# Gates made head by head, and the gates of one of five dense token blocks added in DRAM by indirect DMA

## What is computed

```python
q = (xb @ w_q).reshape(t, PEER_HEADS, 2, PEER_HALF)
s = jnp.einsum('thpd,hpkd->thpk', q, sub_keys)
s1, i1 = lax.top_k(s[:, :, 0], PEER_TOPK)          # 8 heads, 16 of 128 keys in each half
s2, i2 = lax.top_k(s[:, :, 1], PEER_TOPK)
...                                                # the best 16 of the 16 x 16 sums: top_s, idx
gate = jax.nn.softmax(top_s, axis=-1)
act = jax.nn.gelu(jnp.einsum('thkd,td->thk', jnp.take(expert_u, idx, axis=0), xb))
return jnp.einsum('thk,thkd->td', gate * act, jnp.take(expert_v, idx, axis=0))
```

## Time and profile before

| | |
|---|---|
| timed runs | 2938.82 us median of 3 (2930.64 to 2947.14) |
| profiled execution | span 2939.3 us; no time of its own is listed beside the span |
| busy | PE 2830.0 us (96%), DVE 2512.5 (85%), ACT 885.5 (30%), POOL 1029.0 (35%) |
| DMA | 917.54 MB, mean 312 GB/s |
| queues | q1 (SP) 37.3% of 16 engines, q0 (POOL) 36.4%, q10 (ACT) 7.9% |

### The profile page before, as it was taken

How to read it: one execution, slowest core, us unless ns; L and a number is a source line. 1 busy time by engine, 2 the same in 40 slices (tenths; PEclk the granted TensorE clock), 3 DMA queues, 4 the chain that set the end, 5 groups by cost and what they waited for, 6 DMA issues and landing times. The chain is left out here.

```text
span 2939.3 us, 47358 instructions
## 1 busy us (share of the span) xinstructions
PE 2830.0 (96%) x19184; PEld 1834.9 (62%) x19184; DVE 2512.5 (85%) x4708; ACT 885.5 (30%) x1321; POOL 1029.0 (35%) x778
## 2 busy tenths in 40 slices
PE   4999999998999999999999999999999999999998
PEld 4566686766667877677776677777544444444443
DVE  6876556987887879999999999998699999999877
ACT  3333532221111432222222344444222222222223
POOL 0000000002776025444554532222456566655410
PEclk9999999999999999999999999999999999999999
DMA  8989653433999458888888999999999999999972
GB/s 328 348 318 381 238 199 129 144 123 115 391 392 378 192 215 288 303 325 314 330 315 320 354 327 346 350 346 341 368 398 405 405 388 414 407 401 404 364 267 115
DMA packets 222971, 917.54 MB, mean 312 GB/s; under 512 B 20208, under 2 KB 61216, under 8 KB 181536
## 3 DMA queue, kind: packets, MB, share of 16 engines
q1 hardware_dynamic: 61664, 427.91, 37.3%
q0 software_dynamic: 110592, 402.70, 36.4%
q10 hardware_dynamic: 50496, 83.89, 7.9%
HBM read 771.79 MB, written 142.63 MB: 311 GB/s over the span
## 5 line engine op out<-in xcount | busy, mean ns | idle before, releaser
L1718 PE MATMUL psU<-hB,w 128*128 128x320 f16 (+2 forms) x3104 | 927.4, 299 | 27.4 <-ACT Z L753 15.9
L1719 PE MATMUL psU<-hB,w 128*128 128x320 f16 (+2 forms) x3104 | 927.3, 299 | 0.0
L1720 PE MATMUL psU<-hB,w 128*128 128x320 f16 (+2 forms) x3104 | 927.0, 299 | 0.0
L753 ACT ACTIVATE w<-stage 128x2048 f16<-128x2048 f32 x176 | 335.7, 1909 | 606.1 <-PE psX L1720 331.2
L1043 DVE SCALAR_TENSOR_TENSOR w<-stage,w 128x2048 f16<-128x2048 f32 x176 | 402.3, 2287 | 99.4 <-ACT w L753 99.4
L746 POOL DMA_INDIRECT rows<-in_u_rows,idx_sp x200 | 267.8, 1339 | 376.0 <-DVE rows L1139 233.5
L1718 PEld LDWEIGHTS psU<-hB,w 128*128 128x128 f16 x3104 | 304.9, 98 | 140.2 <-issue 22.9
L1720 PEld LDWEIGHTS psU<-hB,w 128*128 128x128 f16 x3104 | 305.1, 98 | 117.6
L1719 PEld LDWEIGHTS psU<-hB,w 128*128 128x128 f16 x3104 | 305.0, 98 | 110.4
L746 POOL DMA_INDIRECT rows<-in_v_rows,idx_sp x205 | 271.4, 1324 | 285.4 <-DVE rows L1139 184.5
L1718 PE MATMUL psX<-w,Z 128*128 128x512 f16 x768 | 292.2, 381 | 7.6 <-DVE Z L1641 4.2
(11 more groups left out here) (263 smaller groups left out, 4435.8 us busy)
## 6 DMA issues: line engine op xcount, KB each, us to landing
stage<-in_u_units SPq DMA_DIRECT2D x64, 1024.0 KB, 8.8
stage<-in_v_units SPq DMA_DIRECT2D x64, 1024.0 KB, 8.0
stage<-in_w_front SPq DMA_DIRECT2D x48, 1024.0 KB, 8.6
hl_dram<-w SPq DMA_DIRECT2D x48, 1024.0 KB, 6.5
w<-hl_dram SPq DMA_DIRECT2D x48, 1024.0 KB, 7.2
a_dram<-R ACTq DMA_DIRECT2D x64, 640.0 KB, 8.0
...
Z<-a_dram SPq DMA_DIRECT2D x32, 1280.0 KB, 11.8
```

The lines of the kernel that those rows point to most:

```text
L753: return nc.scalar.activation(dst, src, func, scale=scale)
L1718: mm(ps, lhs[0](k), rhs[0](k), start=start and s == 0, stop=False)
L1719: mm(ps, lhs[0](k), rhs[1](k), start=False, stop=False)
L1720: last = mm(ps, lhs[1](k), rhs[0](k), start=False, stop=stop and s == n - 1)
```

## The change

Set B's five blocks are parted. Four of them (512 tokens, `NV`) keep the spreading by one-hots, now in 16 units, E44 to E59 (`E_SPREAD` = 44, `N_SPREAD` = 16). The last block (`DS` = 1, 128 tokens) gets its gates by adding: G of that block is a tensor of its own in DRAM, `gs_dram` (8 MB), which ACT zeroes in 16 stores of 512 KB from unit V2 of set B on; then POOL issues 8 x 16 = 128 indirect DMAs, each of which adds 128 gates (one per token, 4 bytes each) at the places i2 * 16384 + i1 * 128 + token. Adds of a head wait for all adds of the head before it to land, since two heads may hit one place. `ADD_AT` deals them out: from E8 on one ahead of every second row step (of units E only, none in Q), from E44 on ahead of every row step, with three row steps without an add at each change of head. They end in E56: 82 lie ahead of E44 and 46 in E44 to E56.

So that a head's gates exist early, they are made head by head: at E(5h+1) DVE shifts head h behind that unit's ranking pieces, ACT takes its Exp after E(5h+2), and at E(5h+3) DVE makes its indices and gates. Head 7 has E36, E37 and E38.

The load of G for two groups becomes two DMAs, one of 2048 KB and one of 512 KB in runs of 512 bytes; `product` becomes five instructions (four over 512 values, one over 4 x 128). POOL fills a zero tile at the start. The ranking itself keeps its units (`E_RANK` = 36). With the spreading four units later, E37 and E39 have six row steps and not four, and units W have four row steps fewer in all.

```diff
@@ -44,6 +44,10 @@
 HB = NT // 2
+DS = 1
+DV = DB - DS
+NV = DV * P
+TS = DS * P
 NGRP = 32
@@ -173,8 +177,8 @@
 X_IDX = X_QB + HEADS * QT["B"]
-X_G = X_IDX + 6
-X_END = X_G + NT // 4
+X_G = X_IDX + 3
+X_END = X_G + NV // 4
@@ -188,8 +192,14 @@
-N_SPREAD = NT // 32
+N_SPREAD = NV // 32
 E_SPREAD = 2 * NGRP - N_SPREAD - 4
+E_RANK = 36
+ZERO_FIRST, ZERO_N = N_OF["B", "V", 2], 16
+HEAD_SHIFT = {min(5 * h + 1, E_RANK): h for h in range(HEADS)}
+HEAD_EXP = {min(5 * h + 2, E_RANK + 1): h for h in range(HEADS)}
+N_SCATTER = DS * HEADS * TOPK
+SCATTER_FIRST, SCATTER_LAST = 8, 2 * NGRP - 6
@@ -272,6 +282,23 @@
+def _additions():
+    at, head_start = set(), 0
+    for m, (_, _, c) in enumerate(ROWS):
+        _, kind, u = SEC_UNITS[c]
+        if kind != "E" or not SCATTER_FIRST <= u < SCATTER_LAST or len(at) == N_SCATTER:
+            continue
+        if len(at) % TOPK == 0 and head_start < 3:
+            head_start += 1
+        elif u >= E_SPREAD or m % 2:
+            at.add(m)
+            head_start = 0
+    assert len(at) == N_SCATTER
+    return at
+ADD_AT = _additions()
 PLACES = _places()
@@ -433,9 +462,12 @@
-        keys_t16 = zone(15300, 640, F16).rearrange("p (n c t) -> p n c t", c=2, t=2)
-        gates16 = zone(15940, 640, F16).rearrange("p (n c t) -> p n c t", c=2, t=2)
-        g_t = zone(16580, 640)
+        keys_t16 = zone(15300, NV, F16).rearrange("p (n c t) -> p n c t", c=2, t=2)
+        gates16 = zone(15940, NV, F16).rearrange("p (n c t) -> p n c t", c=2, t=2)
+        g_t = zone(16580, NV)
+        at_s = zone(R2 + 13968 + NV, TS, U32)
+        gate_s = zone(R2 + 14608 + NV, TS)
+        zeros = rows[:, 3, :]
         iota_k2 = v3(zone(17220, 128, F16), P)
@@ -445,7 +477,9 @@
-        G_t = [z.rearrange("p (n h j t) -> p n h j t", n=NT // 32, h=2, j=4) for z in (zone(5120, 5120), hB_flat)]
+        G_t = [z[:, 0:8 * NV].rearrange("p (n h j t) -> p n h j t", n=NV // 32, h=2, j=4)
+               for z in (zone(5120, 5120), hB_flat)]
+        G_s = [z[:, 8 * NV:8 * NT].rearrange("p (h j t) -> p h j t", h=2, j=4) for z in (zone(5120, 5120), hB_flat)]
         c_hi = [v3(zone(10240 + 1280 * i, 1280, F16), 4) for i in range(2)]
@@ -463,7 +497,10 @@
         a_dram = nc.dram_tensor("a_dram", [NGRP, P, 4, NT], F32).ap()
-        g_dram = nc.dram_tensor("g_dram", [NGRP // 2, P, NT // 32, 2 * P], F32).ap()
+        g_dram = nc.dram_tensor("g_dram", [NGRP // 2, P, NV // 32, 2 * P], F32).ap()
+        gs_flat = nc.dram_tensor("gs_dram", [NKEYS * P * TS, 1], F32).ap()
+        gs_dram = gs_flat.rearrange("(g j p t) o -> g p j (t o)", g=NGRP // 2, j=8, p=P)
+        gs_zero = gs_flat.rearrange("(z p k c) o -> z p k (c o)", z=ZERO_N, p=P, c=D)
@@ -683,11 +724,15 @@
                                  ).then_inc(g_in[pair % 2], 16)
+                    sp.dma_start(G_s[pair % 2].rearrange("p h j t -> p (h j) t"), gs_dram[pair]
+                                 ).then_inc(g_in[pair % 2], 16)
...
                 sp.wait_ge(g_stored[b], 16 * N_SPREAD // 2)
+            for b in range(DS):
+                sp.wait_ge(gs_added[b], 16 * HEADS * TOPK)
             load_group(0)
@@ -719,6 +764,9 @@
             pool.iota(iota_i[:, :], pattern=[[1, P]], base=0, channel_multiplier=0).then_inc(ident_ready, 1)
+            pool.iota(tok_i[:, :], pattern=[[P, DS]], base=0, channel_multiplier=1).then_inc(ident_ready, 1)
+            pool.memset(zeros, 0.0).then_inc(zeros_ready, 1)
+            pool.wait_ge(zeros_ready, 1)
             for i in range(2):
@@ -727,7 +775,26 @@
             pool.memset(acc_sp[:, :, :], 0.0).then_inc(acc_zeroed, 1)
-            for m, (table, slot, _) in enumerate(ROWS):
+            added = [0]
+            def add_gates(n):
+                for _ in range(min(n, N_SCATTER - added[0])):
+                    h, b, k = added[0] // (DS * TOPK), added[0] // TOPK % DS, added[0] % TOPK
+                    if b == 0 and k == 0:
+                        pool.wait_ge(scatter_ready, h + 1)
+                    if h and k == 0:
+                        pool.wait_ge(gs_added[b], 16 * TOPK * h)
+                    i = b * P + h * TOPK + k
+                    pool.indirect_dma_start(gs_flat, bass.IndirectOffsetOnAxis(ap=at_s[:, i:i + 1], axis=0),
+                                            gate_s[:, i:i + 1], None, compute_op=ALU.add).then_inc(gs_added[b], 16)
+                    added[0] += 1
+            pool.wait_ge(gs_zeroed, 16 * ZERO_N)
+            for m, (table, slot, c) in enumerate(ROWS):
+                _, kind, u = SEC_UNITS[c]
+                if m in ADD_AT:
+                    add_gates(1)
                 r, before, _ = PLACES[m]
@@ -965,6 +1029,11 @@
                     make_hi(m)
+                if ZERO_FIRST <= n < ZERO_FIRST + ZERO_N:
+                    if n == ZERO_FIRST:
+                        act.wait_ge(zeros_ready, 1)
+                    part = gs_zero[n - ZERO_FIRST]
+                    act.dma_start(part, zeros.unsqueeze(1).to_broadcast([P, part.shape[1], D])).then_inc(gs_zeroed, 16)
                 if (x, kind, u) == ("B", "E", 0):
@@ -977,7 +1046,7 @@
                     act.wait_ge(row_used, RANK_ROWS)
-                    indices_out(0, 4)
+                    indices_out(0, 2)
                 if kind == "E":
@@ -992,9 +1061,10 @@
                     activation(gate_sp[:, :], gate_sp[:, :], ACT.Exp).then_inc(s_exp, 1)
-                if (x, kind, u) == ("B", "E", E_SPREAD - 4):
-                    act.wait_ge(s_shift, 2)
-                    activation(s_all["B"], s_all["B"], ACT.Exp).then_inc(s_exp, 1)
+                if kind == "E" and u in HEAD_EXP:
+                    h = HEAD_EXP[u]
+                    act.wait_ge(s_shift, 2 + h)
+                    activation(s_all["B"][:, :, h, :], s_all["B"][:, :, h, :], ACT.Exp).then_inc(s_exp, 1)
                 section_gelu(n)
@@ -1469,6 +1540,36 @@
+            def shift_head(h):
+                s3 = s_all["B"][:, :, h, :]
+                most = rk["B"]["rsum"].rearrange("p (b h) -> p b h", h=HEADS)[:, :, h:h + 1]
+                step(V.tensor_copy(most, s3[:, :, 0:1]))
+                settle()
+                V.tensor_tensor(s3, s3, most.to_broadcast([P, DB, TOPK]), ALU.subtract).then_inc(s_shift, 1)
+            def gates_head(h):
+                s3 = s_all["B"][:, :, h, :]
+                total, inv = (rk["B"][i].rearrange("p (b h) -> p b h", h=HEADS)[:, :, h] for i in ("rsum", "rinv"))
+                for b in range(DS):
+                    i1, i2 = (t["B"][:, DV + b, h, :] for t in (i1_all, i2_all))
+                    step(V.tensor_scalar(i1, i1, float(TS), tok[:, b:b + 1], ALU.mult, ALU.add))
+                    settle()
+                    step(V.scalar_tensor_tensor(i2, i2, float(P * TS), i1, ALU.mult, ALU.add))
+                settle()
+                at = at_s.rearrange("p (b h k) -> p b h k", b=DS, h=HEADS)[:, :, h, :]
+                step(V.tensor_copy(at, i2_all["B"][:, DV:DB, h, :]))
+                dve.wait_ge(s_exp, 2 + h)
+                step(V.tensor_reduce(total, s3, AX_X, ALU.add))
+                settle()
+                step(V.reciprocal(inv, total))
+                settle()
+                V.tensor_tensor(s3, s3, inv.unsqueeze(2).to_broadcast([P, DB, TOPK]), ALU.mult).then_inc(gate_ready, 1)
+                dve.wait_ge(gate_ready, 2 + h)
+                settle()
+                V.memset(unread[:, :], 0.0).then_inc(scatter_ready, 1)
             ranks = {}
@@ -1504,15 +1604,14 @@
                 dve.wait_ge(a_in[g % 2], 16 * (g // 2 + 1))
-                dve.wait_ge(g_in[g // 2 % 2], 16 * (g // 4 + 1))
+                dve.wait_ge(g_in[g // 2 % 2], 32 * (g // 4 + 1))
                 for j in range(4):
-                    a = A_t[g % 2][:, j, :].rearrange("p (n t) -> p n t", n=NT // 32)
-                    ins = V.scalar_tensor_tensor(a, a, AS, G_t[g // 2 % 2][:, :, g % 2, j, :], ALU.mult, ALU.mult)
-                    if j < 3:
-                        step(ins)
-                    else:
-                        settle()
-                        ins.then_inc(prod_ready, 1)
+                    a = A_t[g % 2][:, j, 0:NV].rearrange("p (n t) -> p n t", t=32)
+                    step(V.scalar_tensor_tensor(a, a, AS, G_t[g // 2 % 2][:, :, g % 2, j, :], ALU.mult, ALU.mult))
+                a = A_t[g % 2][:, :, NV:NT]
+                ins = V.scalar_tensor_tensor(a, a, AS, G_s[g // 2 % 2][:, g % 2], ALU.mult, ALU.mult)
+                settle()
+                ins.then_inc(prod_ready, 1)
@@ -1594,16 +1693,17 @@
                     rank_some("B", 0, 9)
-                elif kind == "E" and u < E_SPREAD - 4:
+                elif kind == "E" and u < E_RANK:
                     h = min(1 + (u - 1) // 5, 7)
...
                     dve.wait_ge(h2_ready, 1)
-                if kind == "E" and u == E_SPREAD - 5:
+                if kind == "E" and u == E_RANK - 1:
                     rank_some("B", 7, 9)
-                    shift_scores("B")
```

(15 more changed lines are left out.)

32 lines of the change are left out of this document (17 added, 15 removed).

## The result

The changed kernel takes **2958.9 us** (median of four runs, 2955.8 to 2965.1); the kernel before, run beside it, 2939.3 us (2930.6 to 2947.1). The ratio is 1.0075, 95% interval 1.0049 to 1.0100: 0.75% slower. That is outside the 0.5% that I called no change, and on the other side of the kernel before than the forecast of 2929 us, though inside its range. The profiled execution spans 2957.0 us, 17.7 more than the one of before.

The account below looks back on a forecast made before the run. The prediction took PE to bound the kernel, with DVE setting the end of ranking and the start of spreading. From 2939.3 us, -16.4 - 8.5 + 14 + 1 = -9.9 gave 2929 us, range 2910 to 2962.

Parts of the forecast that it names:

- Four spread units less: Spreading: 16 spread units, not 20; four become plain units of 13.0 us instead of 17.1, -16.4 us.
- So the stall goes: Start of spreading: four more plain units let DVE catch up, so the 8.5 us stall vanishes, -8.5 us.
- The row gathers: POOL in ranking and spreading: 1.3 us per gather or add mostly fits; net +1 us, between -10 and +8.
- Sum for the end of ranking: End of ranking: DVE's shifts and gates 10.2, Exp 2.8, row gathers 1, together +14 us, between +3 and +22.
- hidden: Ranking: row waits take up DVE's new work and PE pays only Exp; -21 us, 2918 us, chance 0.22.
- The early stall of 10.5 us at E2: First heads' units: ACT waits for DVE's shift and PE stands some 10 us; not added to the sum.
- the one at E32: End of ranking: PE pays there for DVE's lag, 6.29 us before the change; paying it earlier cuts the lag.
- The adds on the DMA engines: Spreading: 46 adds of 8 items per engine at 20 ns, less free DMA time, +1 us.
- The rival that priced them like data: Spreading: adds cost as much DMA time as data, 110 ns per item; +23 us, 2962 us, chance 0.20.
- The output stage, 0, bound +10: Output stage: PE bounds it, so cutting G's load in two costs 0, at most +10 us with DMA full.
- PE's wait at the first one-hot: Start of spreading: a sign expected in the changed profile, this wait under 2 us.
- the last of them: Spreading: rows late in E44 to E56 was among the signs that would prove the sum wrong.

Follow-up runs that it names:

- E44: Not a run: a unit of the expert stage, the first of the 16 spread units in the changed kernel.
- E56: Not a run: a spread unit of the expert stage, the one in which the adds end in the changed kernel.
- E36: Not a run: a unit of the expert stage, a plain unit behind the ranking, ahead of the spreading.
- E43: Not a run: a unit of the expert stage, the last plain unit ahead of the spreading in the changed kernel.
- the run with eleven memsets: The changed kernel without adds, eleven small chained memsets on POOL in place of each; ratio 1.0045 to the kernel before.
- the two runs with memsets: The changed kernel with each add replaced by small chained memsets on POOL, five in one and eleven in the other; ratios 1.0015 and 1.0045 to the kernel before.
- E33: Not a run: a unit of the expert stage near the end of ranking; its store was forecast near 1617 us.

## Why the prediction was wrong

Against "-16.4 - 8.5 + 14 + 1 = -9.9" stands +17.7 between the two profiled spans.

*"Four spread units less", -16.4.* Right: plain units of 13.0 us up to about E43, and, from the third on, spread units of 17.1, DVE and PE full as before.

*"So the stall goes", -8.5.* **This step failed**, and with it the sign. DVE's own work in the plain units is 7.4 us as I said, and it would have caught up: without adds PE waits 3.1 us at the first one-hot. But DVE's lag stayed, since its rows came no faster than POOL issued them. The stall grew from 8.5 to (35.1 - 17.1) + (22.4 - 17.1) = 23.3 us. The term was -8.5 and came out +14.8, and the run with eleven memsets shows that POOL's time alone brings most of it.

*The row gathers.* The size behind that. I priced a gather at 1.3 us with its gap, which is the least or the median duration and 0.3 us, and gave the add the same; the mean with its gap was 1.6 and the add's 2.14. I wrote that POOL "would become the bound from 2.8 us per add"; with the gathers at 1.6 the point is (13.0 - 8)/2.5 = 2.0 us in a unit of five rows, and the two runs with memsets stand on either side of it, 1.0 us without loss and 2.3 with. I also made no sum for the plain units behind the ranking, which take 13.0 us and not the 13.4 of a ranking unit, and counted as nothing that DVE must not merely keep up there but gain 20 us or more. Over E36 to E43 POOL is not the bound in the mean, but it has only 10 us in hand, and a POOL that is just fast enough hands DVE its rows at little more than PE's pace. POOL's wait for a head's adds to land, which I also took as nothing, came to 12.5 us in the whole span, 0.9 of it in the stretch from 1603 to 1733 us.

*"Sum for the end of ranking", +14.* Wrong in size, the rival "hidden" had it: E0 to E33 went from 529.4 to 528.1 us. DVE's added work is there (458 against 440 us busy from 1100 to 1573 us), and its waits ahead of rows from 1100 to 1650 us fell from 27 us to 7. The early stall of 10.5 us at E2 came as described, and the one at E32 is gone, which fits that they merged. Nine variants of the change show the same 441.9 us from E5 to E33, which I take for PE's pace.

*"The adds on the DMA engines", +1.* Right in effect: spread units of 17.1 us with up to four adds, 512 items, in each, and some 2 to 7 us of the loss not explained by POOL's time. Queue q0 shows 18432 packets more than without adds and a share of 37.6% where the two kernels without adds have 36.7 and 36.9%, which makes about 25 ns a packet; I took 20. The rival that priced them like data fell, though the time came out near its 2962 us: the number was met by another mechanism.

*The output stage, 0, bound +10.* **This step failed too**, by +23.8 us. I priced the 512-byte packets by the engines' time, "0.4 us per pair", and the engines' time was indeed about that (6 us over 16 pairs). What decided was when the load lands: it shares the engines with the gathers and took 28 us, where the 20 us of the run with 4096-byte packets made nobody wait.

That the time lies inside my range is luck. Two terms were missed upward, by 23.3 and 23.8 us, and the ranking's by 15 us the other way. Of the signs that I named, PE's wait at the first one-hot (15.3 us, not under 2), the store of E33 (1601.65, not 1617) and POOL's time for an add (1.8 us, not 1.2) went against the sum, and rows were late in E44, as the last of them says.
